# Stick-breaking attention: the order of ScalarE's and TensorE's steps in a pipeline over 48 blocks

## The chip, the core and the metric

The kernel runs on one core of a Trainium2 chip. The metric is the device time of one execution in microseconds (us). Engines: TensorE (PE: matmuls; its weight loads are listed apart as PEld), VectorE (DVE), ScalarE (ACT), GpSimd (POOL) and SyncE (SP). PSUM has eight banks of 512 float32 columns in each of 128 partitions; matmuls write there.

## What is computed

The reference is a chain of two blocks of two layers each on a sequence of 1024 rows; its other mixers don't matter here. The change touches only the stick-breaking attention in the third layer, 8 heads of dimension 64:

```python
def stick_breaking(q, k, v):
    ...
    scale = d ** -0.5
    for blk in range(S // SB_BLOCK):
        q0 = blk * SB_BLOCK
        kend = q0 + SB_BLOCK
        z = jnp.einsum('bthd,bshd->bhts', qf[:, q0:kend], kf[:, :kend]) * scale
        ...
        strict = s_idx < t_idx
        log_beta = jax.nn.log_sigmoid(z)
        log_one_minus = jnp.where(strict, jax.nn.log_sigmoid(-z), 0.0)
        suffix = lax.cumsum(log_one_minus, axis=3, reverse=True) - log_one_minus
        w = jnp.where(strict, jnp.exp(log_beta + suffix), 0.0)
        outs.append(jnp.einsum('bhts,bshd->bthd', w, vf[:, :kend]))
    return jnp.concatenate(outs, axis=1)
```

With softplus(z) = log(1 + e^z), the weight of key s for query t is e^(z - sum of softplus over the keys from s up to t).

## The kernel before, in words

The kernel is written out engine by engine, with semaphores by hand; no scheduler orders it. Its stages follow one another: the projections (matmuls split in high and low float32 parts), the attention and scan stages, and a boundary between two layers. The stage of this change lies behind `layer_done` 3 and ends with `layer_done` 4.

The stage works through 48 blocks, each a pair of heads `a`, a group `g` of 512 queries and one tile `kb` of 128 keys. Keys lie on the partitions, queries on the columns. A block on the diagonal has only the columns from its key tile on, so blocks are 512, 384, 256 or 128 columns wide (24, 8, 8 and 8 of them), for each of the two heads. The list `blocks` interleaves the chains of two groups and of two head pairs, so a wide block mostly alternates with a narrower one: 512, 384, 512, 256, 512, 128 and so on. `decays` holds all blocks but the first of each chain (`kb` 0), 40 of them.

For each block n these operations are done, with their names and lines:

- PE `stick_scores` (L1508 to L1523): the scores z of both heads into one of three PSUM places (`z_at`, n modulo 3). On the diagonal (32 blocks) a pair of bf16 matmuls (L1518) first writes the mask. It waits for `weight_ready` of block n-3, which used the same place.
- DVE, in its step n: the scores clipped at 30 from above into `SE` (a TENSOR_SCALAR), `low_ready`.
- ACT: the exponential of `SE` in place, then its logarithm with bias 1 (`ln_ready`).
- DVE `stick_softplus` (a TENSOR_TENSOR, the maximum of z and the logarithm) into `SSP`, `sp_ready`.
- PE `stick_sums` (L1525): the running sums over keys, subtracted from z in place (L1530), `logs_summed`; and, for blocks in `decays`, the totals over the keys into one bank, `T_BANK` (L1537), which waits for ACT's decay of the block before in that list (`decay_out`).
- ACT `stick_weights`: the exponential of that, from PSUM into `SPT`, `weight_ready`. ACT `stick_decay`: e^-total, for blocks in `decays`, `decay_out`.
- PE `stick_values` (L1540, L1549): weights times values into one bank. It waits for `weight_ready` of its block and until DVE has taken the block before out of the bank (`block_taken`).
- DVE `stick_decayed` and `stick_add`: the accumulator times the decay, then plus the block's values.

The engines run these in steps of their own. DVE's step n, which the change doesn't touch, is:

```python
            for n in range(len(blocks) + 4):
                if n >= 4:
                    stick_add(n - 4)
                if n < len(blocks):
                    w = 512 - cols_of(n)
                    dve.wait_ge(z_ready, 2 * (n + 1))
                    v.tensor_scalar(SE[n % 2][:, :, 0:w], z_at(n)[:, :, 0:w], SOFTPLUS_IS_Z, None, ALU.min).then_inc(low_ready, 1)
                if 1 <= n <= len(blocks):
                    stick_softplus(n - 1)
                if 3 <= n < len(blocks) + 3:
                    stick_decayed(n - 3)
```

PE's step n issues scores of n, sums (and totals) of n-2, values of n-3. ACT's step n is exponential of n, weights of n-2, logarithm of n, decay of n-2. On ACT and DVE the operations go through a helper (`InOrder`, line 169) that makes each wait for the end of the one before it on its engine, so all of them have line 169 in the profile; they are told apart by form: clipping and softplus of a 512 wide block are 128x1024 (two heads), a decay 128x512. In the listings of the trace each float32 matmul of this stage stands as two passes, so that the two heads make "x4".

Of the kernel before, what the change touches and what calls it, by code (L numbers as in the profile page):

```python
# [173 lines left out]
def build(nc, A, out):  # L174

    with ExitStack() as ctx:
# [140 lines left out]
        def set_ring(pe, size):  # L317

            for bank in range(size, ring["size"]):
                bank_is_free(pe, bank)  # L320
            ring["size"], ring["next"] = size, 0
# [13 lines left out]
        def view(eng, key):  # L335

            u, _, _, place = units[key]
            eng.wait_ge(unit_ready, u + 1)
            return place
# [10 lines left out]
        def landed(eng, *keys):  # L350

            for key in keys:
                _, b, n, _ = units[key]
                eng.wait_ge(ev[b], n)
# [63 lines left out]
        for n in range(2):  # L418
            add(f"h_out{n}", rows_by_tile(h_out, 512 * n, 512 * n + 512))
        chunk_at = {name: n for n, (name, _) in enumerate(chunks)}  # L420

        def slot_view(n):
# [208 lines left out]
        def top_units(m):  # L631
            return 5 if has_tail(groups[m][0]) else 4
# [8 lines left out]
        for m in range(len(groups) - 1):  # L641
            done = last_step[m] - 2
            for u in range(top_units(m + 1)):
                n = done - top_units(m + 1) + 1 + u
# [110 lines left out]
        blocks = []  # L755
# [9 lines left out]
        def cols_of(n):  # L765
            _, g, kb = blocks[n]
            return P * max(0, kb - 4 * g)

        def z_at(n):
            o = 512 * (2 + 2 * (n % 3))  # L770
            return PS[:, o:o + 1024].rearrange("p (h c) -> p h c", h=2)
# [46 lines left out]
        def _(pe):  # L818
# [689 lines left out]
            def stick_scores(n):  # L1508

                a, g, kb = blocks[n]  # L1510
                c0 = cols_of(n)
                w = 512 - c0
                z = z_at(n)
                if n >= 3:
                    pe.wait_ge(weight_ready, n - 2)
                if kb >= 4 * g:
                    for i in range(2):
                        mm(z[:, i, 0:P], STRICT_BF, ID_BF, start=True, stop=False, skip_group_check=True)  # L1518
                for i in range(2):
                    r = 64 * i  # L1520
                    last = mm(z[:, i, 0:w], SKT[r:r + 64, a, kb * P:(kb + 1) * P], SQT[r:r + 64, a, 512 * g + c0:512 * g + 512],
                              start=kb < 4 * g, stop=False, skip_group_check=True)
                    last.then_inc(z_ready, 1)  # L1523

            def stick_sums(n):  # L1525

                w = 512 - cols_of(n)
                pe.wait_ge(sp_ready, n + 1)
                for i in range(2):
                    last = mm(z_at(n)[:, i, 0:w], LOWER, SSP[n % 2][:, i, 0:w], start=False, stop=True, skip_group_check=True)  # L1530
                last.then_inc(logs_summed, 1)
                if n in decays:
                    k = decays.index(n)
                    if k:
                        pe.wait_ge(decay_out, k)
                    for i in range(2):
                        last = mm(T_BANK[64 * i:64 * i + 64, 0:w], ONES[:, 0:64], SSP[n % 2][:, i, 0:w], start=True, stop=True)  # L1537
                    last.then_inc(total_ready, 1)

            def stick_values(n):  # L1540

                a, g, kb = blocks[n]
                w = 512 - cols_of(n)
                pe.wait_ge(weight_ready, n + 1)
                if n:
                    pe.wait_ge(block_taken, n)
                for i in range(2):
                    h = 2 * a + i
                    last = mm(B_BANK[64 * i:64 * i + 64, 0:w], SV[:, kb, h * SD:(h + 1) * SD], SPT[n % 2][:, i, 0:w], start=True, stop=True)  # L1549
                last.then_inc(block_ready, 1)  # L1550

            pe.wait_ge(lower_ready, 1)
            for n in range(len(blocks) + 3):
                if n < len(blocks):
                    stick_scores(n)
                if 2 <= n < len(blocks) + 2:
                    stick_sums(n - 2)
                if n >= 3:
                    stick_values(n - 3)
            pe.wait_ge(block_taken, len(blocks))  # L1560
            set_ring(pe, BANKS)
            pe.sem_inc(layer_done, 1)
# [130 lines left out]
        def _(act):  # L1693
# [191 lines left out]
            for u, name in enumerate(e_halves):  # L1885
                what, n = divmod(u, 2)
# [229 lines left out]
            def stick_weights(n):  # L2116
                w = 512 - cols_of(n)
                act.wait_ge(logs_summed, n + 1)
                if n >= 2:
                    act.wait_ge(block_ready, n - 1)  # L2120
                f(SPT[n % 2][:, :, 0:w], z_at(n)[:, :, 0:w], ACT.Exp).then_inc(weight_ready, 1)

            def stick_decay(n):
                if n in decays:
                    k, w = decays.index(n), 512 - cols_of(n)
                    act.wait_ge(total_ready, k + 1)
                    if k >= 2:
                        act.wait_ge(decayed_acc, k - 1)
                    f(SF[k % 2][:, 0:w], PS[:, 512:512 + w], ACT.Exp, scale=-1.0).then_inc(decay_out, 1)

            for n in range(len(blocks) + 2):
                if n < len(blocks):
                    e = SE[n % 2][:, :, 0:512 - cols_of(n)]
                    act.wait_ge(low_ready, n + 1)
                    f(e, e, ACT.Exp)
                if n >= 2:
                    stick_weights(n - 2)
                if n < len(blocks):
                    f(e, e, ACT.Ln, bias=1.0).then_inc(ln_ready, 1)
                if n >= 2:  # L2140
                    stick_decay(n - 2)
# [99 lines left out]
            for t in range(NL):  # L2241
                for s in range(NS):
                    n = t * NS + s
# [1101 lines left out]
```

## Time and profile before

| | |
|---|---|
| median of 3 runs | 2767.04 us (2765.52 to 2770.16) |
| the profiled execution | 2770.5 us, of which its span 2768.7 us |
| PE busy, of the span | 2566.3 us (93%) |
| DVE, ACT, POOL busy | 1419.2, 1153.6, 381.1 us |
| mean granted TensorE clock | 0.969 of full speed |
| DMA | 139.73 MB, mean 50 GB/s |

The profile lists instructions with the time that each was busy, and for the idle time before one what ended it ("<-"). A matmul's end is modelled, and consecutive ones overlap in the records, so prices are better read from start to start. The granted clock is TensorE's: 1.00 is 2.4 GHz, 0.50 is 1.2 GHz, and what lies between is a stretch with both in it. The names in the rows are memories: `PS` is PSUM, `HT` holds `SE`, `SSP`, `SPT` and the accumulators.

### The profile page before, as it was taken

To read this page: it belongs to the slowest core of one execution; us is meant where nothing else is said; L and a number is where in the kernel's file an instruction comes from. 1 tells how busy PE (TensorE), PEld (TensorE's weight loads), DVE (VectorE), ACT (ScalarE), POOL (GpSimd) and SP (SyncE) were. 2 spreads that over 40 slices of the span, in tenths; PEclk is the share of its full clock that TensorE was granted. 3 is DMA by queue.
4 is the path that set the end of the run, shared out by engine and by line. 5 is a ranking of instruction groups with operands and counts; after the bars stand their busy time and mean duration, and the time that the engine had idled before them with its cause. 6 is when DMAs were issued, how large, how long until landed. Compare 5 with 4: busy or idle time off the path is not lost. (4 is left out here: it accounts for less than half of the span.)

```text
span 2768.7 us, 38552 instructions
## 1 busy us (share of the span) xinstructions
PE 2566.3 (93%) x14759; PEld 1979.2 (71%) x14759; DVE 1419.2 (51%) x2283; ACT 1153.6 (42%) x1977; POOL 381.1 (14%) x415
## 2 busy tenths in 40 slices
PE   4999998999999999989999999899998999999787
PEld 3778987877778878933337778786334877798776
DVE  5113265666655514666764723411777547265752
ACT  6112344454454321134443622311767647333662
POOL 1000020010020000046761000000000010004710
PEclk8999999999999999989999999999999999998889
DMA  7430010000112131110002220102000220111012
GB/s 257 174 139 24 18 33 1 1 1 1 62 54 91 47 61 46 32 37 1 1 1 91 92 78 30 59 3 76 1 1 24 84 88 31 38 47 62 1 54 76
DMA packets 87991, 139.73 MB, mean 50 GB/s; under 512 B 19513, under 2 KB 54738, under 8 KB 87682
## 3 DMA queue, kind: packets, MB, share of 16 engines
q1 hardware_dynamic: 70592, 75.90, 8.8%
q0 software_dynamic: 16976, 61.30, 6.2%
q8 instruction: 120, 1.97, 0.3%
q14 instruction: 61, 0.50, 0.1%
q10 hardware_dynamic: 242, 0.07, 0.0%
HBM read 120.47 MB, written 16.78 MB: 50 GB/s over the span
## 5 line engine op out<-in xcount | busy, mean ns | idle before, releaser
L169 ACT ACTIVATE WORK<-PS 128x512 f32<-128x512 f32 (+5 forms) x309 | 152.6, 494 | 659.2 <-PE PS L863 388.7
L863 PE MATMUL PS<-HT_R,W_R 128*128 128x512 f32 (+1 forms) x896 | 334.3, 373 | 0.0
L862 PE MATMUL PS<-WORK_R,W_R 128*128 128x512 f32 (+1 forms) x736 | 271.4, 369 | 0.0
L861 PE MATMUL PS<-WORK_R,W_R 128*128 128x512 f32 (+1 forms) x672 | 250.0, 372 | 14.4 <-DVE W_R L169 9.9
L169 ACT ACTIVATE HT<-PS 128x1024 f32<-128x1024 f32 (+6 forms) x211 | 156.0, 739 | 161.0 <-PE PS L1296 126.4
L989 PE MATMUL PS<-WORK_R,HT_R 128*128 128x512 f32 x528 | 210.3, 398 | 8.8 <-DVE W_R L169 7.5
L863 PE MATMUL PS<-W_R,WORK_R 128*128 128x256 f32 (+3 forms) x704 | 215.2, 306 | 0.0
L990 PE MATMUL PS<-WORK_R,MIXT_R 128*128 128x512 f32 x544 | 214.1, 394 | 0.0
L991 PE MATMUL PS<-W_R,HT_R 128*128 128x512 f32 x528 | 207.4, 393 | 0.0
L862 PE MATMUL PS<-W_R,HT_R 128*128 128x256 f32 (+2 forms) x688 | 206.2, 300 | 0.0
L926 PE MATMUL PS<-BASE,WORK 128*128 128x128 f32 (+1 forms) x1186 | 175.2, 283 | 25.3 <-DVE WORK L169 16.8
L863 PEld LDWEIGHTS PS<-HT_R,W_R 128*128 128x128 f32 x896 | 170.8, 191 | 29.9
L926 PEld LDWEIGHTS PS<-BASE,WORK 128*128 128x128 f32 (+1 forms) x1186 | 137.7, 143 | 54.7 <-issue 17.7
L861 PE MATMUL PS<-W_R,WORK_R 128*128 128x256 f32 (+2 forms) x560 | 169.0, 302 | 2.9 <-issue 1.4
L169 DVE TENSOR_TENSOR W_R<-W,W_R 128x1024 fp32r<-128x1024 f32 (+2 forms) x76 | 86.9, 1165 | 162.7 <-ACT W_R L169 143.5
L861 PEld LDWEIGHTS PS<-WORK_R,W_R 128*128 128x128 f32 x672 | 128.5, 191 | 43.8 <-issue 23.5
L169 DVE COPY WORK<-PS 128x512 f32<-128x512 f32 (+1 forms) x101 | 61.3, 607 | 191.7 <-PE PS L863 103.6
L862 PEld LDWEIGHTS PS<-WORK_R,W_R 128*128 128x128 f32 x736 | 140.6, 191 | 22.4 <-issue 0.5
L169 ACT ACTIVATE MIXT<-PS 128x512 f32<-128x512 f32 (+1 forms) x76 | 43.7, 575 | 262.4 <-PE PS L863 236.3
L169 ACT ACTIVATE WORK<-WORK 128x1024 f32<-128x1024 f32 (+2 forms) x88 | 78.9, 897 | 153.8 <-DVE WORK L169 149.2
L863 PEld LDWEIGHTS PS<-W_R,WORK_R 128*128 128x128 f32 x704 | 134.6, 191 | 3.9
L862 PEld LDWEIGHTS PS<-W_R,HT_R 128*128 128x128 f32 x688 | 132.1, 192 | 2.5
(328 smaller groups left out, 5587.3 us busy)
## 6 DMA issues: line engine op xcount, KB each, us to landing
MIXT<-in_w_mod POOLq DMA_DIRECT2D x8, 2048.0 KB, 8.7
x_scratch<-WORK POOLq DMA_DIRECT2D x24, 512.0 KB, 2.9
WORK<-x_scratch POOLq DMA_DIRECT2D x24, 512.0 KB, 3.6
W<-in_odd_w_in SPq DMA_DIRECT2D x12, 1024.0 KB, 5.2
W<-in_even_w_in SPq DMA_DIRECT2D x5, 2048.0 KB, 7.9
W<-in_w_mod SPq DMA_DIRECT2D x4, 2048.0 KB, 20.8
WORK<-in_x POOLq DMA_DIRECT2D x16, 512.0 KB, 8.7
W<-in_e_w_in SPq DMA_DIRECT2D x6, 1024.0 KB, 5.9
```

The source lines that it names most:

```text
L169: self.last = Signalled(self, issue(*args, **kwargs))
L861: mm(out, a[0], b_[0], start=k == 0, stop=False)
L862: mm(out, a[1], b_[0], start=False, stop=False)
L863: return mm(out, a[0], b_[1], start=False, stop=k == KT - 1)
L926: last = nc.tensor.transpose(bank[0:m, n * P:n * P + a.shape[0]], a, IDENT[0:a.shape[0], 0:a.shape[0]])
L989: mm(bank, high, wh, start=k == 0, stop=False)
L990: mm(bank, low, wh, start=False, stop=False)
L991: last = mm(bank, high, wl, start=False, stop=k == KT - 1)
```

## The change

On PE the scores of block n are issued at the end of step n, behind the sums of n-2 and the values of n-3. On ACT the weights of block n-2 are issued at the start of step n, ahead of the exponential of n.

```diff
@@ -1551,12 +1551,12 @@
 
             pe.wait_ge(lower_ready, 1)
             for n in range(len(blocks) + 3):
-                if n < len(blocks):
-                    stick_scores(n)
                 if 2 <= n < len(blocks) + 2:
                     stick_sums(n - 2)
                 if n >= 3:
                     stick_values(n - 3)
+                if n < len(blocks):
+                    stick_scores(n)
             pe.wait_ge(block_taken, len(blocks))
             set_ring(pe, BANKS)
             pe.sem_inc(layer_done, 1)
@@ -2129,13 +2129,12 @@
                     f(SF[k % 2][:, 0:w], PS[:, 512:512 + w], ACT.Exp, scale=-1.0).then_inc(decay_out, 1)
 
             for n in range(len(blocks) + 2):
+                if n >= 2:
+                    stick_weights(n - 2)
                 if n < len(blocks):
                     e = SE[n % 2][:, :, 0:512 - cols_of(n)]
                     act.wait_ge(low_ready, n + 1)
                     f(e, e, ACT.Exp)
-                if n >= 2:
-                    stick_weights(n - 2)
-                if n < len(blocks):
                     f(e, e, ACT.Ln, bias=1.0).then_inc(ln_ready, 1)
                 if n >= 2:
                     stick_decay(n - 2)
```

How the engines' instructions stand around blocks 8 and 9, PE first. Step 8 before (mask and scores of 8, sums and totals of 6, values of 5), and the start of step 9:

```order
L1518 MATMUL PS<-BF 128x128 [waits stick_weight_ready]
L1518 MATMUL PS<-BF 128x128
L1521 MATMUL PS<-WORK 128x512 x2
L1530 MATMUL PS<-HT 128x512 [waits stick_sp_ready]
L1530 MATMUL PS<-HT 128x512
L1537 MATMUL PS<-HT,ONES 64x512 [waits stick_decay_out]
L1537 MATMUL PS<-HT,ONES 64x512
L1549 MATMUL PS<-HT,WORK 64x256 [waits stick_block_taken,stick_weight_ready]
L1549 MATMUL PS<-HT,WORK 64x256
L1521 MATMUL PS<-WORK 128x512 [waits stick_weight_ready]
L1521 MATMUL PS<-WORK 128x512
L1530 MATMUL PS<-HT 128x128 [waits stick_sp_ready]
```

After the change, step 8 and the start of step 9:

```order
L1530 MATMUL PS<-HT 128x512 [waits stick_sp_ready]
L1530 MATMUL PS<-HT 128x512
L1537 MATMUL PS<-HT,ONES 64x512 [waits stick_decay_out]
L1537 MATMUL PS<-HT,ONES 64x512
L1549 MATMUL PS<-HT,WORK 64x256 [waits stick_block_taken,stick_weight_ready]
L1549 MATMUL PS<-HT,WORK 64x256
L1518 MATMUL PS<-BF 128x128 [waits stick_weight_ready]
L1518 MATMUL PS<-BF 128x128
L1521 MATMUL PS<-WORK 128x512 x2
L1530 MATMUL PS<-HT 128x128 [waits stick_sp_ready]
L1530 MATMUL PS<-HT 128x128
L1537 MATMUL PS<-HT,ONES 64x128 [waits stick_decay_out]
```

The mask and scores of block 8 (L1518, L1521) moved from ahead of the sums of block 6 (L1530) to behind the values of block 5 (L1549); the sums of block 7, 128 wide, now follow the scores of block 8 at once.

ACT, steps 8 and 9, before (exponential, weights, logarithm, decay):

```order
L169 ACTIVATE HT<-HT 128x1024 [waits stick_decay_out,stick_low_ready]
L169 ACTIVATE HT<-PS 128x1024 [waits act_step,stick_block_ready,stick_logs_summed]
L169 ACTIVATE HT<-HT 128x1024 [waits stick_weight_ready]
L169 ACTIVATE HT<-PS 128x512 [waits stick_ln_ready,stick_decayed_acc,stick_total_ready]
L169 ACTIVATE HT<-HT 128x1024 [waits stick_decay_out,stick_low_ready]
L169 ACTIVATE HT<-PS 128x2x128 [waits act_step,stick_block_ready,stick_logs_summed]
L169 ACTIVATE HT<-HT 128x1024 [waits stick_weight_ready]
L169 ACTIVATE HT<-PS 128x128 [waits stick_ln_ready,stick_decayed_acc,stick_total_ready]
```

And after the change:

```order
L169 ACTIVATE HT<-PS 128x1024 [waits stick_decay_out,stick_block_ready,stick_logs_summed]
L169 ACTIVATE HT<-HT 128x1024 [waits stick_weight_ready,stick_low_ready]
L169 ACTIVATE HT<-HT 128x1024 [waits act_step]
L169 ACTIVATE HT<-PS 128x512 [waits stick_ln_ready,stick_decayed_acc,stick_total_ready]
L169 ACTIVATE HT<-PS 128x2x128 [waits stick_decay_out,stick_block_ready,stick_logs_summed]
L169 ACTIVATE HT<-HT 128x1024 [waits stick_weight_ready,stick_low_ready]
L169 ACTIVATE HT<-HT 128x1024 [waits act_step]
L169 ACTIVATE HT<-PS 128x128 [waits stick_ln_ready,stick_decayed_acc,stick_total_ready]
```

The operation from `PS` that waits for `stick_logs_summed`, the weights, moved ahead of the one that waits for `stick_low_ready`, the exponential; exponential and logarithm of a block now stand side by side.

## Rows read from the trace of the kernel before

**Rows 1.** The page: busy time, share of the span and instructions of each engine.
```profile
PE 2566.3 (93%) x14759; PEld 1979.2 (71%) x14759; DVE 1419.2 (51%) x2283; ACT 1153.6 (42%) x1977; POOL 381.1 (14%) x415
```

**Rows 2.** A stretch of the stage: PE, PEld, DVE, ACT, POOL busy, clock, DMA, GB/s.
```profile
1945.00:2100.00 155.00, 142.10 (x622) 53.96 (x620) 112.04 (x147) 106.97 (x143) 0.00 (x0) 1.00 0.00 1
```

**Rows 3.** Waits, 1925 to 2131 us: waiting line, releaser, us, times, longest.
```profile
ACT HT L169 <- DVE HT L169: 51.1, 42, 4.0
PEld PS L1518 <- ACT HT L169: 36.6, 31, 2.4
```

**Rows 4.** Timeline of blocks 8 and 9: start us, us, engine, line, operation.
```profile
1958.21 1.98 PE L1530 MATMUL PS<-HT 128*128 128x512 f32 x4
1958.36 1.22 DVE L169 TENSOR_SCALAR HT<-PS 128x1024 f32<-128x1024 f32 x1 [0.15 <-PE PS L1521]
...
1959.62 1.06 ACT L169 ACTIVATE HT<-HT 128x1024 f32<-128x1024 f32 x1 [2.01 <-DVE HT L169]
1959.71 0.42 DVE L169 TENSOR_TENSOR HT<-PS,HT 128x256 f32<-128x256 f32 x1
...
1960.13 1.08 PE L1537 MATMUL PS<-HT,ONES 128*64 128x512 f32 x4
...
1960.79 1.02 ACT L169 ACTIVATE HT<-PS 128x1024 f32<-128x1024 f32 x1
1961.04 0.60 PE L1549 MATMUL PS<-HT,WORK 128*64 128x256 f32 x4
...
1961.84 1.06 ACT L169 ACTIVATE HT<-HT 128x1024 f32<-128x1024 f32 x1
...
1961.87 1.13 PE L1521 MATMUL PS<-WORK 64*128 64x512 f32 x4 [0.23 <-ACT HT L169]
...
1963.01 0.60 ACT L169 ACTIVATE HT<-PS 128x512 f32<-128x512 f32 x1
1963.07 1.23 DVE L169 TENSOR_SCALAR HT<-PS 128x1024 f32<-128x1024 f32 x1 [0.96 <-PE PS L1521]
...
1963.66 0.44 PE L1537 MATMUL PS<-HT,ONES 128*64 128x128 f32 x4
```

**Rows 5.** Timeline at the stage's start: block 0 goes from DVE to PE.
```profile
1931.13 1.23 DVE L169 TENSOR_TENSOR HT<-PS,HT 128x1024 f32<-128x1024 f32 x1
...
1932.41 1.98 PE L1530 MATMUL PS<-HT 128*128 128x512 f32 x4 [1.83 <-DVE HT L169]
1932.46 1.22 DVE L169 TENSOR_SCALAR HT<-PS 128x1024 f32<-128x1024 f32 x1
```

**Rows 6.** Timeline at the stage's end: sums, totals, values 128 wide.
```profile
2126.80 0.71 PE L1530 MATMUL PS<-HT 128*128 128x128 f32 x4
...
2127.44 0.44 PE L1537 MATMUL PS<-HT,ONES 128*64 128x128 f32 x4
...
2127.71 0.60 PE L1549 MATMUL PS<-HT,WORK 128*64 128x256 f32 x4
```

**Rows 7.** Group by form, 1925 to 2131 us: busy us, mean ns, idle before.
```profile
L1518 PE MATMUL PS<-BF 128*128 128x128 bf16 x64 | 9.2, 227 | 14.4 <-ACT HT L169 13.9
```

**Rows 8.** Timeline: the clippings of blocks 21 and 47.
```profile
2013.32 1.22 DVE L169 TENSOR_SCALAR HT<-PS 128x1024 f32<-128x1024 f32 x1 [0.96 <-PE PS L1521]
...
2121.79 0.42 DVE L169 TENSOR_SCALAR HT<-PS 128x256 f32<-128x256 f32 x1
```

**Rows 9.** PE's timeline in other stages, with its idle time in brackets.
```profile
925.17 0.36 PE L861 MATMUL PS<-W_R,MIXT_R 128*128 128x256 f32 x1 [2.55 <-DVE W_R L169]
...
2586.03 1.11 PE L926 MATMUL PS<-BASE,HT 128*128 128x128 f32 x4 [3.56 <-DVE HT L169]
```

**Rows 10.** Stretches behind idle times of rows 5 and 9, columns as in rows 2.
```profile
1933.00:1945.00 12.00, 10.29 (x34) 3.08 (x33) 6.97 (x7) 8.34 (x10) 0.00 (x0) 1.00 0.01 4
...
926.00:929.00 3.00, 3.00 (x16) 3.00 (x15) 2.79 (x3) 0.21 (x1) 0.00 (x0) 0.50 0.00 0
...
2588.00:2592.00 4.00, 4.00 (x22) 4.00 (x22) 3.15 (x5) 1.18 (x2) 2.78 (x4) 0.55 0.00 0
```

## Prediction

> **What bounds the kernel now.** The page comes first: TensorE (PE) is busy for 93% of the run [rows 1], which says little about a single stage. The stage is that of stick-breaking attention, 48 blocks between about 1926 and 2130 us. Read by itself it has PE busy for 142.1 of 155 us, VectorE (DVE) for 112.0, ScalarE (ACT) for 107.0, the clock granted in full and no DMA [rows 2]. The list of waits then names a ring, not an engine: ACT waits 51.1 us for DVE, and PE's weight loads in front of the score matmuls wait 36.6 us for ACT [rows 3].
>
> The timeline shows the ring at blocks 8 and 9, both 512 columns wide [rows 4]. DVE clips the scores of block 8 at 1958.36. ACT takes the exponential at 1959.62. ACT's weights of block 6 follow at 1960.79 and end at 1961.81. PE's scores of block 9 (L1521) start at 1961.87 and name ACT as what they waited for. Their clipping starts at 1963.07, 4.71 us after the one before. The sum is 1.23 + 0.03 + 1.06 + 0.11 + 1.02 + 0.06 + 1.20 = 4.71. The sums of block 6 (L1530, 1958.21) ran meanwhile and waited for nothing, since DVE had written its softplus one step earlier.
>
> **What the change removes.** On ACT the weights of block n-2 now stand ahead of the exponential of block n. They don't wait for the clipping of n any more, so weights leave the ring: 1.02 + 0.11 us of the 4.71 would go. Nothing is added on any engine. No DMA is in the stage.
>
> **What it adds.** PE's step n is now sums of n-2, totals of n-2, values of n-3, scores of n. The sums need the softplus of n-2. DVE's order isn't changed: it writes that softplus in its step n-1, behind the clipping of block n-1, which needs the scores of n-1. Those are the last thing of PE's step n-1. So PE ends a step with scores, has nothing else it may do, and waits until DVE has clipped them and written one softplus. Only then come sums, totals, values and the next scores. In the kernel before, that wait lay behind the scores of the next block and was covered by them. Now all four parts of PE's work stand in the ring in series. Queued behind the waiting sums are the totals, the values and the scores, and DVE's next clipping waits for the latter.
>
> The prices, from start to start at 512 columns: clipping to softplus 1.35 (1958.36 to 1959.71), sums 1.92 (1958.21 to 1960.13), totals 0.91 (1960.13 to 1961.04), values I price as the totals, whose form (64 columns of weights, 512 moved) they share, and scores to their clipping 1.20 [rows 4]. Softplus to sums took 1.28 for an operation of 1.23, so the handoff costs 0.05 [rows 5]. At 128 columns sums take 0.64 and totals 0.27 [rows 6], the masking matmul pair ahead of 32 of the 48 blocks' scores some 0.2 [rows 7], and a clipping 0.42 [rows 8]. Between 512 and 128 I go in a straight line: sums 1.92, 1.49, 1.07, 0.64.
>
> One step with both blocks wide is then 1.35 + 1.28 + 1.92 + 0.91 + 0.91 + 1.20 = 7.6 us where 4.7 stood. Most steps have a narrower block in them. A second leg ends last where block n is wide and n-1 narrow: the totals of n-1 reuse one PSUM bank and need ACT's decay of n-2 first (as L1537 at 1963.66, 0.05 behind the decay that ended at 1963.61). From the clipping's end that leg is 0.03 + 1.17 + 1.17 + 0.60 + 0.05 = 3.0 us for exponential, logarithm and decay [rows 4], against 0.12 + 0.42 + 0.05 + 0.64 = 1.2 for softplus and sums of a 128 wide block.
>
> I add this up over one chain of twelve steps, blocks 9 to 20, whose pattern the next chain repeats. Six clippings of 512 and two each of 384, 256 and 128: 11.5 us. The longer of the two legs: 3.3 in the six steps behind a 512 wide block (0.12 + 1.23 + 0.05 + 1.92), softplus and sums again with 2.6 and 1.9 in two behind narrower ones, and the decay leg with 3.0 in two, 2.6 and 2.7 in two more, in all 35.7. Totals, ten blocks: 6.5. Values, twelve blocks: 8.3. Scores up to the clipping, with eight masks: 13.6. The sum is 75.6 us. The trace has 50.25 for the same steps (1963.07 [rows 4] to 2013.32 [rows 8]). That is +25.4 for twelve, and for the 45 steps from 1932.46 [rows 5] to 2121.79 [rows 8] +95. The start loses 3 more: the clipping of block 2 now stands behind the sums of block 0 (1.9 us) and its own scores (1.2). The end of the stage keeps its chain.
>
> **The clock.** Each step now has a stretch in which PE idles: between two wide blocks 0.15 + 1.35 + 1.28 = 2.8 us, with a narrow one in it 2.0 to 2.5, and where the decay ends last 1 to 1.8 more behind short sums. In the trace an idle time of 1.83 us left the clock full (1.00 from 1933 to 1945 us), but one of 2.55 us was followed by a stretch at 0.50, the lower of the two levels (1.2 GHz), and one of 3.56 us by 0.55 [rows 5, 9, 10]. The new idle times lie between these. The Trainium skill, "TensorE: Matmul & The Clock Gate", section "A second HAM failure mode: psum-queue depth-cycling", says that short idles between groups of matmuls, frequent enough, make the clock swing between its levels. By that rule the swing comes, without it this term is nothing; for one such idle the trace agrees.
>
> At half clock PE's work takes twice as long, and it is all in the ring. The half-clock stretch behind the 2.55 us idle holds at least the 3 us of its row, that behind 3.56 at least 4 [rows 10]. With such stretches of 3 to 5.5 us, and work in nearly all of it, one fall loses 1.5 to 2.7 us. I take 2.2 (an estimate) and a fall in two steps of three: 30 x 2.2 = 66 us. The bounds are none, and the clock down throughout: sums, totals, values and scores are 17.9 + 6.5 + 8.3 + 13.6 = 46.3 us of a chain, some 42 outside the cover of the decay leg, so 3.75 x 42 = 158 us more.
>
> **The sum.** The profiled execution took 2770.5 us, 3.5 above the median of the runs. 2770.5 + 95 + 3 + 66 = 2934.5, and I forecast 2935. A difference under 0.2% (5.5 us) could not be told from none here.
>
> **The rivals.** First, the clock stays full, since the idle of 1.83 did no harm and all new ones but the wide pairs' are nearer to it than to 3.56: 2770.5 + 98 = 2869. Second, the clock is down nearly all the time, as repeated falls leave no time to rise: 2770.5 + 98 + 158 = 3027. Third, faster: the softplus is ready when the sums ask for it, so only the removal counts. PE's own work bounds then. A chain's 46.3 us of PE work against 50.25 saves 4, over 45 steps 15 us: 2756. It decides at the point where DVE writes the softplus of n-2 ahead of the clipping of n-1; DVE's program doesn't do that, and the waits on both sides are by name, so I see no way there. Fourth, no change: each engine's work is the same as before and only its order moves, so whoever takes the busiest engine for the bound expects 2770. The Trainium skill, "Perfetto Trace Analysis", section "Identifying the Most-Contended Engine", says to take the engine of highest occupancy, and to judge TensorE by its weight loads instead. By that rule the bound here is DVE, 112.0 of 155 us (weight loads: 54.0), none of its work changes, and the time stays. The trace speaks against it: DVE itself waited for PE's L1521 before the clippings of blocks 8 and 9 [rows 4], so its work is a link of a ring and not the bound.
>
> **How the numbers follow.** Ring and swinging clock: 0.62. Ring at full clock: 0.20. Clock mostly down: 0.12. Faster: 0.03. No change: 0.03. The range goes from the full clock rival, with 12 us for its sum's error, to the clock falling in every step and half the way on to staying down: 2857 to 2995. What is left out is most of the second rival, the third and the fourth. Faster by over 0.2%: 0.03, within: 0.03, slower: 0.94.
>
> **What would show it.** In the profile after, PE's waits at L1530 should name DVE in nearly all of 48 blocks, 2 to 2.8 us each, and its waits for ACT at L1518 and L1521 be gone. Clippings of two wide blocks should stand 7.6 us apart at full clock, the narrow steps 5.3 to 6.8. Some L1537 should wait for ACT. The stage should last 300 to 370 us instead of 204, and the stages behind it be moved, not changed. ACT's weights should start as soon as the sums end. I'm wrong about the ring if L1530 doesn't wait, about the decay leg if L1537 never names ACT, and about the clock if its mean in the stage is above 0.95 or under 0.6.

## The result, and the profile after

| | median | runs | against before |
|---|---|---|---|
| before | 2767.32 us | 2765.52 to 2770.16 (4) | |
| the change | 2918.48 us | 2908.27 to 2928.24 (4) | 1.0539, interval 1.0502 to 1.0576 |

The change makes the kernel 5.4% slower, 151 us. 2935 was forecast, with a range from 2857 to 2995. The profiled execution took 2908.27 us.

The page's first lines after the change, to be held against [rows 1]:

```profile
span 2906.5 us, 38552 instructions
...
PE 2608.5 (90%) x14759; PEld 1984.9 (68%) x14759; DVE 1417.9 (49%) x2283; ACT 1154.3 (40%) x1977; POOL 382.1 (13%) x415
```

No engine's instruction count has changed. PE's busy time has grown by 42 us, with the same matmuls: part of them ran at the lower clock. A stretch of the stage, with the columns of [rows 2] (PE, PEld, DVE, ACT and POOL busy, clock, DMA, GB/s):

```profile
1950.00:2200.00 250.00, 165.12 (x566) 57.55 (x565) 102.98 (x136) 98.84 (x132) 0.00 (x0) 0.85 0.00 0
```

PE is busy for 66% of it where it was 92%, and the clock is 0.85 of full speed where it was 1.00. The waits of the stage (waiting line, releaser, us in total, times, longest), to be held against [rows 3]:

```profile
DVE HT L169 <- PE PS L1521: 186.2, 46, 5.8
PEld PS L1530 <- DVE HT L169: 135.6, 48, 4.3
ACT HT L169 <- DVE HT L169: 130.6, 47, 4.9
PE PS L1530 <- DVE HT L169: 102.9, 47, 2.7
ACT HT L169 <- PE PS L1530: 69.0, 33, 3.7
...
PE PS L1537 <- ACT HT L169: 14.0, 12, 1.6
...
PEld PS L1518 <- ACT HT L169: 8.0, 12, 0.8
```

PE waits for DVE before the sums (L1530) in 47 of the 48 blocks, 102.9 us, 2.2 each on average. DVE waits for PE's scores (L1521) 186.2 us. The mask's weight loads (L1518) wait 8.0 us for ACT where it was 36.6 [rows 3], and before the masks and scores themselves PE has no wait for ACT in the list any more. So the old ring is nearly gone, but 14.0 us at the totals (L1537) for ACT's decay are new. The ring is visible in one step at full clock, blocks 11 and 12 (start us, us, engine, line):

```profile
1999.47 1.13 PE L1521 MATMUL PS<-WORK 64*128 64x512 f32 x4
2000.67 1.23 DVE L169 TENSOR_SCALAR HT<-PS 128x1024 f32<-128x1024 f32 x1 [2.88 <-PE PS L1521]
...
2002.03 0.96 DVE L169 TENSOR_TENSOR HT<-PS,HT 128x768 f32<-128x768 f32 x1
...
2003.04 1.56 PE L1530 MATMUL PS<-HT 128*128 128x384 f32 x4 [2.44 <-DVE HT L169]
...
2004.53 0.87 PE L1537 MATMUL PS<-HT,ONES 128*64 128x384 f32 x4
...
2005.22 1.03 PE L1549 MATMUL PS<-HT,WORK 128*64 128x512 f32 x4
2005.22 0.14 PEld L1549 LDWEIGHTS PS<-HT,WORK 128*64 128x64 f32 x2 [0.18 <-issue]
2006.18 0.11 PEld L1518 LDWEIGHTS PS<-BF 128*128 128x128 bf16 x2 [0.81 <-ACT HT L169]
2006.18 0.29 PE L1518 MATMUL PS<-BF 128*128 128x128 bf16 x2
...
2007.18 0.69 DVE L169 TENSOR_SCALAR HT<-PS 128x512 f32<-128x512 f32 x1 [2.60 <-PE PS L1521]
```

Clipping of block 11 at 2000.67, softplus of block 10 at 2002.03, its sums at 2003.04, totals at 2004.53, values of block 9 at 2005.22, the next clipping at 2007.18: 6.51 us in all, 6.43 by the working ahead. The step from the clipping of block 21 to that of block 22, with blocks 20 and 21 both wide, has the same order and, in part, the lower clock (the last three rows are stretches, with the columns of [rows 2]):

```profile
2070.07 0.44 PE L1537 MATMUL PS<-HT,ONES 128*64 128x128 f32 x4 [1.62 <-ACT HT L169]
...
2074.11 1.23 DVE L169 TENSOR_SCALAR HT<-PS 128x1024 f32<-128x1024 f32 x1 [5.37 <-PE PS L1521]
...
2075.47 1.23 DVE L169 TENSOR_TENSOR HT<-PS,HT 128x1024 f32<-128x1024 f32 x1
...
2076.74 3.17 PE L1530 MATMUL PS<-HT 128*128 128x512 f32 x4 [2.71 <-DVE HT L169]
...
2079.85 1.54 PE L1537 MATMUL PS<-HT,ONES 128*64 128x512 f32 x4
...
2082.74 0.96 DVE L169 TENSOR_SCALAR HT<-PS 128x768 f32<-128x768 f32 x1 [4.46 <-PE PS L1521]
```

```profile
2074.00:2077.00 3.00, 0.29 (x3) 0.26 (x2) 2.66 (x3) 1.60 (x2) 0.00 (x0) 1.00 0.00 0
2077.50:2080.50 3.00, 3.00 (x5) 0.63 (x5) 0.69 (x1) 0.83 (x3) 0.00 (x0) 0.50 0.01 3
2081.00:2083.50 2.50, 1.67 (x12) 0.55 (x8) 0.76 (x1) 0.00 (x0) 0.00 (x0) 1.00 0.00 0
```

From 2074.11 to the next clipping at 2082.74 it takes 8.63 us, where the legs at full clock give 6.93. Sums start 2.63 us behind the clipping's start as foreseen, but they take 3.11 us until the totals instead of 1.92, and the totals 1.37 instead of 0.91. The clock was still 1.00 through the idle time of 2.71 us before the sums, and fell after they had begun.

From the clipping of block 2 to that of block 47 the profiled run takes 331.5 us (1931.19 to 2262.70), where before it took 189.3 ([rows 5] to [rows 8]): 142.2 more. Read in slices of a quarter of a microsecond, the clock falls to the lower level 26 times between those two clippings and spends 95.6 us there, 3.7 us each time on average. PE is busy for about 89 of those 95.6 us. The same reading is used for the clock's time in the experiments below.

From block 0's clipping to block 2's it takes 10.5 us instead of 4.8. The other stages are some 10 us shorter in this execution than in the one before, which no part of the change explains. It is also the fastest of the four runs of the changed kernel.

### The profile page after: what moved, and what is told of

Read it like the earlier page. It is cut to its first block and busy times, and to the rows that moved or that the text cites. A ratio compares the mean times of both kernels' runs of the same rounds, so it can differ in the third digit from the quotient of the medians.

```text
span 2906.5 us, 38552 instructions
## 1 busy us (share of the span) xinstructions
PE 2608.5 (90%) x14759; PEld 1984.9 (68%) x14759; DVE 1417.9 (49%) x2283; ACT 1154.3 (40%) x1977; POOL 382.1 (13%) x415
## 5 line engine op out<-in xcount | busy, mean ns | idle before, releaser
L1530 PE MATMUL PS<-HT 128*128 128x512 f32 (+3 forms) x192 | 103.4, 673 | 102.9 <-DVE HT L169 102.9
L169 ACT ACTIVATE HT<-HT 128x1024 f32<-128x1024 f32 (+3 forms) x136 | 105.1, 773 | 139.1 <-DVE HT L169 134.0
L169 DVE COPY WORK<-PS 128x512 f32<-128x512 f32 (+1 forms) x101 | 61.3, 607 | 191.3 <-PE PS L863 103.7
L1530 PEld LDWEIGHTS PS<-HT 128*128 128x128 f32 x192 | 38.4, 228 | 157.5 <-DVE HT L169 135.6
```

The costliest lines, as they stand in the source:

```text
L169: self.last = Signalled(self, issue(*args, **kwargs))
```

## The experiments

All are made from the kernel before or from the changed one. Ratios are to runs of the kernel before on the same chip.

### TensorE's order alone

The kernel before with only the first half of the diff:

```diff
-                if n < len(blocks):
-                    stick_scores(n)
                 if 2 <= n < len(blocks) + 2:
                     stick_sums(n - 2)
                 if n >= 3:
                     stick_values(n - 3)
+                if n < len(blocks):
+                    stick_scores(n)
```

> TensorE's order of the change alone, ScalarE as before (exponential, weights, logarithm, decay). Ring theory: the whole loss comes from TensorE's order, so this is as slow as the change or slower: the weights now lie in the decay leg, which becomes 1.05 us longer where it ends last, by my sum over the 45 steps 14 us in all: 2932 (2915 to 2950). Rival (ScalarE's new order is what costs, since its weights block the exponential): near the kernel before, 2767.

Measured: 2955.56 us (2949.42 to 2961.34), ratio 1.0679 (1.0662 to 1.0697). The whole loss, and 37 us more, is in TensorE's order. That is 24 above the expected value and 6 above its range. In the list of its waits, and in a stretch of its stage:

```profile
PE PS L1537 <- ACT HT L169: 27.2, 12, 2.8
```

```profile
1950.00:2200.00 250.00, 163.92 (x503) 56.65 (x502) 91.28 (x119) 87.75 (x117) 0.00 (x0) 0.77 0.00 0
```

PE waits 27.2 us at the totals where it is 14.0 with the full change: 13.2 more, the longer decay leg as sized. From clipping 2 to clipping 47 this kernel takes 370.0 us, 38.5 more than the changed one. The clock is at its lower level for 170.7 us of it instead of 95.6, and PE is busy for 142.7 of them instead of 89. If a busy microsecond there loses half of itself, that is 27 us more (an estimate), so leg and clock together give the 38.5. Why the clock stays down so much longer here was not tested.

### ScalarE's order alone

```diff
             for n in range(len(blocks) + 2):
+                if n >= 2:
+                    stick_weights(n - 2)
                 if n < len(blocks):
...
                     f(e, e, ACT.Exp)
-                if n >= 2:
-                    stick_weights(n - 2)
-                if n < len(blocks):
                     f(e, e, ACT.Ln, bias=1.0).then_inc(ln_ready, 1)
```

> ScalarE's order of the change alone, TensorE as before. Ring theory: the weights leave the ring of the kernel before and a shorter one is left, scores of n, sums of n-2, weights of n-2, scores of n+1: 1.06 + 1.98 + 0.1 + 1.02 + 0.06 = 4.2 us for wide blocks instead of 4.7; TensorE's own work (46.3 of 50.25 us in twelve steps) bounds the gain at 15 us: 2752 to 2764. Rival (ScalarE's new order costs, because weights wait for sums and hold up the exponential): slower than 2767, up to 2900.

Measured: 2761.41 us (2758.25 to 2763.88), ratio 0.9975 (0.9966 to 0.9983). This half of the change is a gain of 7 us by itself, clear of the noise. Behind TensorE's new order the same edit is worth more: the full change is 37 us below the kernel of the section before. PE's waits for ACT at the mask have shrunk from 13.9 us to 2.1, while some at the totals have come:

```profile
PE PS L1537 <- ACT HT L169: 8.0, 11, 0.9
...
PE PS L1518 <- ACT HT L169: 2.1, 4, 1.1
```

```profile
1945.00:2100.00 155.00, 146.64 (x643) 56.04 (x643) 116.70 (x155) 111.53 (x148) 0.00 (x0) 1.00 0.00 1
```

PE is busy for 146.6 of 155 us at full clock, against 142.1 [rows 2]. What is left to gain in the stage is small.

### TensorE's idle time filled with extra matmuls

The changed kernel with this ahead of the sums. The place `z_at(n)` is free there and is overwritten by the scores of n, so the products are never read; the kernel does 8 x 45 matmuls more:

```diff
             for n in range(len(blocks) + 3):
+                if 3 <= n < len(blocks):
+                    pe.wait_ge(weight_ready, n - 2)
+                    for i in range(8):
+                        mm(z_at(n)[:, i % 2, :], STRICT_BF, BF[:, :], start=True, stop=True, skip_group_check=True)
                 if 2 <= n < len(blocks) + 2:
                     stick_sums(n - 2)
```

> The change, plus eight 512-column bf16 matmuls in each step from 3 on (1.7 us at full clock, into the PSUM place that the next scores overwrite), put into TensorE's idle time ahead of the sums; they are extra work whose results are overwritten. Clock theory: falls of the clock cost the change some 45 us (331.5 us measured from clipping 2 to 47 against 286 by the ring at full clock); with the idle filled the clock stays up, and more work gives less time: 2873 (2865 to 2885). Rival (the clock follows and costs nothing, or the 45 us are other waits): 2918 or slower.

Measured: 2874.62 us (2871.66 to 2875.08), ratio 1.0384 (1.0368 to 1.0400). More work took 44 us less. PE's timeline in one step (block 10's scores, the filler at L1557, the sums), and a stretch of the stage:

```profile
1991.72 0.92 PE L1521 MATMUL PS<-WORK 64*128 64x384 f32 x4
1992.57 1.90 PE L1557 MATMUL PS<-BF 128*128 128x512 bf16 x8
1995.08 1.98 PE L1530 MATMUL PS<-HT 128*128 128x512 f32 x4 [0.61 <-DVE HT L169]
```

```profile
1950.00:2200.00 250.00, 223.00 (x968) 84.36 (x966) 118.30 (x155) 114.02 (x151) 0.00 (x0) 1.00 0.00 1
```

In this step the filler ends inside the idle time: the sums still wait 0.61 us for DVE. That it holds nothing up elsewhere either is seen at steps that the changed kernel ran at full clock too. From clipping to clipping, those of blocks 10 to 11, 11 to 12 and 15 to 16 take 6.71, 6.51 and 5.90 us there and 6.71, 6.51 and 5.91 here. The clock is 1.00 and PE busy for 89%. From clipping 2 to clipping 47 this kernel takes 288.8 us (1938.36 to 2227.11 in its timeline), against 284.3 by the prediction's sum (189.3 + 95; the expectation has 286) and 331.5 in the changed kernel. So 42.7 us of the 142.2 are the clock's, and 99.4 the ring's. Half of the 89 us that PE was busy at the lower level comes to 44.5, by another way nearly the same. The chain of twelve steps, blocks 9 to 20, takes 76.26 us here, against 75.6 in the prediction's sum.

### The decay ahead of the exponential

```diff
                 if n >= 2:
                     stick_weights(n - 2)
+                if n >= 2:
+                    stick_decay(n - 2)
                 if n < len(blocks):
...
                     f(e, e, ACT.Ln, bias=1.0).then_inc(ln_ready, 1)
-                if n >= 2:
-                    stick_decay(n - 2)
```

> The change, with ScalarE's decay of n-2 moved ahead of the exponential of n (weights, decay, exponential, logarithm). Decay-leg theory: the totals no longer wait for ScalarE behind exponential and logarithm, the leg over softplus and sums is left in every step: 16 us less by my sum at full clock, and some more if shorter idles spare falls of the clock: 2895 (2885 to 2905). Rival (the decay is hidden anyway): 2918.

Measured: 2894.91 us (2893.77 to 2901.72), ratio 1.0465 (1.0450 to 1.0480). PE's waits for ACT at the totals have left the list of waits, those for DVE at the sums are 102.9 us as before. The second leg was real, and 24 us went with it, 20.3 of them between clippings 2 and 47 (311.3 us). Part of it is the clock's, which is 0.88 from 1950 to 2200 us and at its lower level for 78.5 us instead of 95.6. The next section parts the two.

### The filler and the early decay together

Both edits above in one kernel, to see whether the parts add up.

> The change, with the filler matmuls and with ScalarE's decay ahead of the exponential. If the ring at full clock is the sum of its legs, what is left is 2770 + 98 - 16 = 2852 (2846 to 2862): the filler takes the clock's part away and the early decay the second leg. Rival (the filler holds up the sums where the decay no longer does): 2875.

Measured: 2857.59 us (2856.47 to 2859.16), ratio 1.0321 (1.0306 to 1.0337).

```profile
1950.00:2200.00 250.00, 234.50 (x1017) 88.79 (x1016) 124.22 (x164) 119.23 (x160) 0.00 (x0) 1.00 0.00 1
```

At full clock the early decay alone is worth 17 us between the medians (2874.6 to 2857.6), against 16 by the legs. Inside the stage it is less: from clipping 2 to clipping 47 the two traces have 288.8 and 276.0 us, a difference of 12.8, and 0.8 more at the start. Of the 20.3 us in the section before, then, 12.8 are the leg's and some 7.5 the clock's. The expected value is 6 too low, as it was 2 too low for the filler kernel. So ring, decay leg and clock are terms that add up, to within some 4 us.

### Values behind the scores

TensorE's step in the order sums, scores, values, the rest as changed:

```diff
                 if 2 <= n < len(blocks) + 2:
                     stick_sums(n - 2)
-                if n >= 3:
-                    stick_values(n - 3)
                 if n < len(blocks):
                     stick_scores(n)
+                if n >= 3:
+                    stick_values(n - 3)
```

> The change, with TensorE's step in the order sums, scores, values. Ring theory: the values (31.9 us over 45 steps) leave the ring, since they run while VectorE clips and writes the softplus, and TensorE's idle gets shorter by as much, so that most falls of the clock (some 45 us) are spared: 2918 - 32 - 30 = 2856 (2835 to 2880). Rival (the loss comes from sums ahead of scores alone): 2918.

Measured: 2862.24 us (2856.26 to 2862.62), ratio 1.0333 (1.0315 to 1.0351), 56 us below the change.

```profile
PE PS L1530 <- DVE HT L169: 57.5, 42, 2.7
```

```profile
1950.00:2200.00 250.00, 183.96 (x694) 61.34 (x692) 125.42 (x165) 119.71 (x159) 0.00 (x0) 0.92 0.00 0
```

The line is from the waits up to 2190 us; over the whole stage they are 61.3 us. PE waits that long for DVE at the sums instead of 102.9, since the values now run in that time, and the clock is 0.92. From clipping 2 to clipping 47 it takes 276.7 us, 54.8 fewer, and the clock is at its lower level for 54.6 us instead of 95.6, with PE busy in 51.8 of them instead of 89. By half of the busy time some 19 us of the 54.8 are the clock's and 36 the ring's, where 30 and 32 were expected: the total was right, and its parts less so.

### Softplus ahead of the clipping on VectorE

The changed kernel, with DVE's step reordered. This is the point that the third rival of the prediction named.

```diff
+                if 1 <= n <= len(blocks):
+                    stick_softplus(n - 1)
                 if n < len(blocks):
                     w = 512 - cols_of(n)
...
-                if 1 <= n <= len(blocks):
-                    stick_softplus(n - 1)
```

> The change, with VectorE's softplus of n-1 ahead of its clipping of n (the point that the third rival named). Ring theory: TensorE's sums find their softplus ready, the 97 us of the ring and the 45 us of the clock go, and another ring ends last: clipping, exponential, logarithm, softplus of the same block and then the next clipping, 1.23 + 0.03 + 1.17 + 1.17 + 1.35 = 4.95 us for a wide block and 179 us over 45 steps against 189 in the kernel before, some more where TensorE's own order adds to it: 2770 (2755 to 2800). Rival (TensorE's series of four parts costs by itself, whatever VectorE does): above 2860.

Measured: 2842.06 us (2836.95 to 2843.48), ratio 1.0263 (1.0248 to 1.0279): between the two theories, 42 us above my range. The waits of the whole stage say what I had left out:

```profile
DVE HT L169 <- PE PS L1521: 89.0, 43, 4.3
...
PE PS L1537 <- ACT HT L169: 56.5, 25, 3.6
```

PE's waits for DVE at the sums have shrunk from 102.9 to 4.1 us. It waits 56.5 us at the totals for ACT's decay instead, which still stands behind exponential and logarithm. With the first leg of the ring gone the second one closes it, as the next run shows. The clock is not full either: 0.90 from 1950 to 2200 us.

### Softplus ahead of the clipping, and the decay ahead of the exponential

Both edits in one kernel.

> The change, with VectorE's softplus ahead of its clipping and ScalarE's decay ahead of the exponential. With the first of the two alone the time was 2842 where I expected 2770, and TensorE waited 54.2 us at L1537 for ScalarE's decay; I had left that leg out (clipping, exponential, logarithm, decay, totals, values, scores, 7.2 us for wide blocks). If that leg is all that held it, this gives what I expected of the swap: 2770 (2755 to 2795). Rival (TensorE's series of parts is a ring of its own there): 2820 or more.

Measured: 2789.84 us (2789.44 to 2791.71), ratio 1.0078 (1.0061 to 1.0095).

```profile
DVE HT L169 <- ACT HT L169: 30.4, 35, 2.2
...
PE PS L1549 <- DVE HT L169: 22.6, 21, 1.5
```

```profile
1950.00:2100.00 150.00, 128.89 (x538) 46.66 (x538) 99.93 (x132) 94.24 (x125) 0.00 (x0) 1.00 0.00 1
```

With both legs opened, 129 of the 151 us are gone although PE's order is still that of the change. The clock is full again. What is left is, for the wide blocks, the ring that was expected of the swap: DVE waits 30.4 us for ACT's logarithm, and a step that begins with a wide clipping takes 4.8 us on average, as the 4.95 expected. But those that begin with a narrow one take 4.4, where the expectation had them much shorter. The 45 steps take 207.0 us and not 179, and the median lies 20 above the expected value, though in its range. What holds the narrow steps was not isolated; the values' waits for DVE, 22.6 us, are new there. With TensorE's new order the kernel is 21 us slower than the one before in company with these orders of DVE and ACT, and 151 with those of the change. The same two orders with TensorE's old one were not run, so how the 21 us divide stays open.

### TensorE's order alone, with the filler

> TensorE's order of the change alone (ScalarE as before), with the eight filler matmuls of the other filler run in each step. That order alone took 2956, 24 more than I expected. If the excess is the clock's, the filler takes clock and excess away and leaves the ring with its longer decay leg: 2770 + 98 + 14 = 2882 (2875 to 2895). Rival (the excess is the leg over ScalarE): above 2900.

Measured: 3025.90 us (3024.46 to 3026.52), ratio 1.0930 (1.0915 to 1.0945). Neither theory, since in this kernel the filler holds up the sums:

```profile
2002.10 1.06 ACT L169 ACTIVATE HT<-HT 128x1024 f32<-128x1024 f32 x1 [6.78 <-DVE HT L169]
...
2003.27 1.02 ACT L169 ACTIVATE HT<-PS 128x1024 f32<-128x1024 f32 x1
...
2004.35 3.51 PE L1557 MATMUL PS<-BF 128*128 128x512 bf16 x8 [3.58 <-ACT HT L169]
...
2007.65 0.72 PE L1530 MATMUL PS<-HT 128*128 128x128 f32 x4
```

The filler (L1557) must wait for the weights of the block whose PSUM place it writes. With ACT's old order these come behind the exponential of the next block (2002.10, then 2003.27 to 2004.29), so the filler starts at 2004.35 and the sums stand behind it until 2007.65. It didn't hold the clock up either, which is 0.85 from 1950 to 2200 us. The run therefore says nothing on the clock's share in TensorE's order alone. It does show what a wait at the head of a step costs: all that is queued behind it, here 70 us.

### The best of the parts

The kernel before, with ACT's step in the order weights, decay, exponential, logarithm, and TensorE and VectorE untouched.

> TensorE as in the kernel before, ScalarE's step in the order weights, decay, exponential, logarithm. In the run with ScalarE's order of the change alone TensorE still waited 8.0 us for ScalarE at the totals and 2.1 at the mask. If those waits are on the path, they go: 2752 (2748 to 2757). Rival (the decay is now in front of the exponential and takes from it what the totals gain): 2761.

Measured: 2756.07 us (2753.36 to 2756.79), ratio 0.9955 (0.9942 to 0.9967). It is faster than both kernels, 12 us below the one before. PE's waits for ACT at the totals are gone from its list of waits.

```profile
1950.00:2100.00 150.00, 148.13 (x648) 56.50 (x646) 117.22 (x155) 110.96 (x148) 0.00 (x0) 1.00 0.00 1
```

PE is busy for 148.1 of 150 us: the stage has TensorE's own work for its bound. The chain of blocks 9 to 20 takes 46.24 us, and the prediction's sum of TensorE's work was 46.3. Its third rival, 2756 by that bound, comes to the time of this kernel, whose TensorE order is the old one.

## Why the prediction was right

**What the change removes.** Right: ACT's weights leave the old ring, and that is worth 7 us alone. It was a gain, and it didn't decide.

**What it adds.** Right in mechanism and size. The ring at full clock was put at +95 us over 45 steps; the filler kernel shows +99.4. TensorE's order alone carries the loss, and opening the ring on the other engines takes 129 of the 151 us away. The single steps at full clock agree with the working (6.51 against 6.43 in the step shown above). One sign was wrong: steps of 7.6 us at full clock were named for two wide blocks. That sum also has wide values and wide scores in it. With the narrow blocks that stand around such a pair, no step behind the clipping of block 2 comes to 7.6 at full clock: the step from the clipping of the second of two wide blocks takes 6.99, the longest of all 7.35.

**The decay leg.** Right in mechanism: 16 us by the sum, 17 between the medians at full clock, 12.8 between clippings 2 and 47 of the two traces. The latter is the leg's own price, so the sum put it some 3 us too high, and the rest of the ring too low. It was underrated as a ring of its own only later, in the expectation of the swap.

**The start.** Put at 3 us, measured 5.7: the clock was at its lower level there as well.

**The clock.** The mechanism was right and the term was sized too high: 66 us forecast, 42.7 measured. The forecast was 30 falls, "a fall in two steps of three", and 2.2 us lost by each. The trace has 26 falls, so their number was nearly right; what was mis-sized is the loss of one fall, 42.7 / 26 = 1.6 us. They last 3.7 us on average and not the 4.4 or so that 2.2 us lost stand for, and PE is busy for 93% of that time. The loss is 0.45 us for each microsecond at the lower level. The rule of the Trainium skill on short idles ("TensorE: Matmul & The Clock Gate", section "A second HAM failure mode: psum-queue depth-cycling") held: the longest idle before the sums is 2.7 us, and the clock swings through the whole stage.

The size of the term also moves from run to run. By the times of the four runs (2908.3 to 2928.2) above the filler kernel's median (2874.6) it is 34 to 54 us, and only the fastest run was traced. The forecast lies above all of them.

**The rivals.** The ring at full clock, 2869, is 6 us from what the filler kernel measures (2874.6). The clock mostly down, 3027, didn't come: at its lower level it spent 29% of the time between the two clippings. The rule of the busiest engine (the Trainium skill, "Perfetto Trace Analysis", section "Identifying the Most-Contended Engine"), as the prediction read it, foresaw no change and fell: no engine's work changed, and the time rose by 5.4%. (The section names, beside the weight loads that the prediction used, the share of peak arithmetic as a measure for TensorE.)

**The total.** 95 + 3 + 66 = 164 against 99.4 + 5.7 + 42.7 = 147.8 in the profiled execution's stage, and 151 between the medians. All three terms had the right sign. The ring was 4 too low, the start 3 too low and the clock 23 too high. These errors offset each other in part, and it is by that luck that the total lies nearer than the clock's term. The range, 138 us wide, was as wide as it was because of that term. The other signs came as named: the stage lasts 350 us (1919.5 to 2269.3), L1537 names ACT 12 times, and the clock of 0.85 lies between the two values that would have spoken against it.

## What to carry to other kernels

In a pipeline written by hand over several engines, follow for each order the ring through all engines' steps: what stands last in one engine's step and first in its next one, with another engine's two operations between, puts the whole step in series. A wait that was covered before can become the bound without any instruction being added, so cost a reordering by the ring's sum and not by busy shares. Change one engine's order at a time: here one half alone gave -7 us and the other alone +187, and together they show only +151. Where a reordering leaves TensorE idle for some 2 us in each step, price the clock as a term of its own and give it a wide range: here it was 42.7 us beside 99.4 of the ring.

## What the runs showed of the hardware

Idle times of at most 2.7 us, one or two in each step of 5.4 to 9.3 us, came with a TensorE clock of 0.85 on average, and of 0.77 in the kernel with TensorE's order alone, where steps last up to 9.9 us. Filling 1.9 us of each idle time in the changed kernel with matmuls that compute nothing of use brought the clock to 1.00 and made the kernel 44 us faster. In the step shown, the clock fell after PE had begun to work again and not while it idled. Of the time at the lower level PE was busy for 93%, and each microsecond there cost 0.45.

The changed kernel's four runs lie at 2908, 2911, 2926 and 2928 us, with a mean clock over the run of 0.955, 0.954, 0.948 and 0.947. The two longer ones spent some 40 us more at the lower level, so the same program can meet the clock differently from run to run. It need not: the kernel with TensorE's order and the filler has a clock of 0.85 in the stage as well, and its four runs lie within 2.1 us.
